# Input projections of a two-layer kernel in another order, and the gate's Silu in two halves

## The reference

```python
h = _rmsnorm(x, norm_w)
proj = jnp.einsum('bld,de->ble', h, w_in)
aq, ak, av, az, dq, dk, dv, dz, b_f, a_f, b_b, a_b = _split_proj(proj)
attn = _neighbourhood_attention(rms(aq), rms(ak), av, rpb) * jax.nn.silu(az)      # 8 heads of 64
qkv = jax.nn.silu(_centred_depthwise_conv(concat([dq, dk, dv]), conv_w))          # 4 heads of 128
o_f = _gated_delta_chunked(dq, dk, dv, g_f, beta_f)          # chunks, each with a triangular solve
o_b = flip(_gated_delta_chunked(flip(dq), flip(dk), flip(dv), flip(g_b), flip(beta_b)))
o = o_f + o_b
o = o * lax.rsqrt(jnp.mean(o * o, axis=-1, keepdims=True) + EPS) * dn_norm_w
delta = o * jax.nn.silu(dz)
x = x + jnp.einsum('ble,ed->bld', jnp.concatenate([attn, delta], axis=-1), w_out)
```

## Time and profile before

| what | us |
|---|---|
| median of 3 runs | 2304.66 (2299.58 to 2307.76) |
| span of the profiled execution | 2301.0 |
| from its start to the last input projection's end | 560.0 |
| from there to the first matmul of wo0, at 764.3 | 204.3 |
| from wo0's first matmul to the end | 1536.7 |

### The profile page before, as it was taken

How to read it: one execution, slowest core, us unless ns; L and a number is a source line. 1 busy time by engine, 2 the same in 40 slices (tenths; PEclk the granted TensorE clock), 3 DMA queues, 4 the chain that set the end, 5 groups by cost and what they waited for, 6 DMA issues and landing times.

```text
span 2301.0 us, 29061 instructions
## 1 busy us (share of the span) xinstructions
PE 2206.9 (96%) x11559; PEld 1800.5 (78%) x11559; DVE 1093.5 (48%) x2025; ACT 936.8 (41%) x1705; POOL 380.9 (17%) x596
## 2 busy tenths in 40 slices
PE   8999999898997899999999999999999999999998
PEld 6778777676796688788887788887888888888886
DVE  5454545443256343566555664655514243433441
ACT  4544544343364143456455554543313233232220
POOL 5200112644403110000000000003301111010111
PEclk9999999999598899999999999999999999999999
DMA  4621345353743231111110211112221111344232
GB/s 142 221 82 58 86 127 171 109 149 101 242 157 92 110 124 52 42 49 62 34 59 23 65 56 46 37 46 69 64 66 55 37 56 55 119 140 158 93 105 87
DMA packets 171384, 209.76 MB, mean 91 GB/s; under 512 B 36576, under 2 KB 124752, under 8 KB 169712
## 3 DMA queue, kind: packets, MB, share of 16 engines
q1 hardware_dynamic: 150752, 141.51, 19.6%
q0 software_dynamic: 20496, 66.39, 9.0%
HBM read 150.41 MB, written 53.77 MB: 89 GB/s over the span
## 4 chain that ended last, share of the span: by engine, by line
PE 86%; DVE 5%; ACT 4%; issue 1%; DMA 1%; POOL 1%; SPq 0%; DVEq 0%; POOLq 0%; ACTq 0%
PE PS L1730 12%; PE PS L1732 12%; PE PS L1731 12%; PE PS L1724 9%; PE PS L1726 9%; PE PS L1725 9%; PE PS L1690 5%; PE PS L2018 3%; PE PS L1997 3%; PE PS L1801 2%; PE PS L1827 2%; DVE WH L2439 2%; PE PS L2050 1%; PE PS L2063 1%; DMA RAW<-in_w_in 1%
## 5 line engine op out<-in xcount | busy, mean ns | idle before, releaser
L1730 PE MATMUL PS<-WH,HH 128*128 128x512 f32 x1344 | 546.8, 407 | 19.3 <-DVE WH L2439 10.7
L1732 PE MATMUL PS<-WH,HL 128*128 128x512 f32 x1344 | 528.1, 393 | 0.0
L1731 PE MATMUL PS<-WH,HH 128*128 128x512 f32 x1344 | 527.2, 392 | 0.0
L1724 PE MATMUL PS<-HH,WH 128*128 128x512 f32 (+1 forms) x976 | 399.5, 409 | 4.2 <-DVE WH L2439 4.2
L1726 PE MATMUL PS<-HH,WH 128*128 128x512 f32 (+1 forms) x976 | 382.9, 392 | 0.0
L1725 PE MATMUL PS<-HL,WH 128*128 128x512 f32 (+1 forms) x976 | 382.3, 392 | 0.0
L1730 PEld LDWEIGHTS PS<-WH,HH 128*128 128x128 f32 x1344 | 254.8, 190 | 78.8 <-DVE WH L2439 11.8
L1732 PEld LDWEIGHTS PS<-WH,HL 128*128 128x128 f32 x1344 | 254.0, 189 | 55.2
L2439 DVE SCALAR_TENSOR_TENSOR WH<-RAW,WK,WH 128x512 fp32r<-128x512 f32 (+2 forms) x248 | 188.0, 781 | 221.4 <-ACT WH L2072 220.8
L1731 PEld LDWEIGHTS PS<-WH,HH 128*128 128x128 f32 x1344 | 255.3, 190 | 46.2
L1724 PEld LDWEIGHTS PS<-HH,WH 128*128 128x128 f32 (+1 forms) x976 | 183.0, 187 | 43.7 <-DVE WH L2439 5.7
(11 more groups left out here) (313 smaller groups left out, 2923.2 us busy)
## 6 DMA issues: line engine op xcount, KB each, us to landing
RAW<-in_w_in SPq DMA_DIRECT2D x200, 256.0 KB, 2.9
RAW<-in_w_out SPq DMA_DIRECT2D x32, 256.0 KB, 3.5
sig_d<-WK POOLq DMA_DIRECT2D x32, 256.0 KB, 2.3
WK<-sig_d POOLq DMA_DIRECT2D x32, 256.0 KB, 3.2
WK<-in_rpb POOLq DMA_DIRECT2D x16, 480.0 KB, 5.6
RAW<-in_w_in SPq DMA_DIRECT2D x32, 192.0 KB, 2.6
dnc_d<-TM SPq DMA_DIRECT2D x12, 512.0 KB, 3.6
TM<-dnc_d SPq DMA_DIRECT2D x10, 512.0 KB, 4.6
```

The lines of the kernel that those rows point to most:

```text
L1724: e.matmul(ps, wh, hh, start=k == 0, stop=False)
L1730: e.matmul(ps, hh, wt[:, 0:width], start=k == 0, stop=False)
L1731: e.matmul(ps, hh, wt[:, 512:512 + width], start=False, stop=False)
L1732: mm = e.matmul(ps, hl, wt[:, 0:width], start=False, stop=k == 7)
```

## The change

The blocks come in the order dn0, dn1, dn2, dn3, na0, na1, na2, dz, na3. Delta head 0 is now the block whose six tiles run together. dz is evacuated by ACT with a plain scaled copy into TM[:, 2], the region where `solve` works, so it waits for the inverse's last stores; then Silu (ACT) and the norm weights (POOL) are applied in place to four tiles at a time, each half with one store. In the plan dz waits for ("da", 1). Pair 3's attention is set free only after na3, like the other pairs', and its V is gathered on POOL in one part.

```diff
-X = ["dz", "dn0", "dn1", "dn2", "na0", "dn3", "na1", "na2", "na3"]
+X = ["dn0", "dn1", "dn2", "dn3", "na0", "na1", "na2", "dz", "na3"]
+    def waiting(held):
+        return held and held[:2] == ("tile", 0) and ("g", *held[1:], 7) in plan.known and ("ev", *held[1:]) not in plan.known
-        if ring[state["n"] % len(ring)] == state["open"]:
+        while ring[state["n"] % len(ring)] == state["open"] or waiting(holder.get(ring[state["n"] % len(ring)])):
     def first_out(b):
-        for t in range(8):
-            yield has("xs")
-            yield has("g", b, t, 7)
-            slot(("ev", b, t), "stg", 3)
-            put("ev", b, t)
-            plan.now[0] += 1200.0
-            if t in (1, 3):
-                yield
-                put("xb", t // 2)
-            yield
-        put("dg")
+        yield has("xs")
+        for th in range(2):
+            put("xb", th)
+            yield
+        put("dg")
+        for c in range(3):
+            if c == 2:
+                yield has("co", 0, 0)
+            for th in range(2):
+                yield has("g", b, (c, th), 7)
+                put("ev", b, (c, th))
+                yield
+            plan.spawn(conv(0, c))
...
+                if b == 0:
+                    plan.drain(has("xb", 1))
+                put("ev", b, t)
...
-        if p == 3:
-            yield has("d9", 1, 14)
         if ("no", p, 1 - h, 7) in plan.known and ("nw", p) not in plan.known:
             put("nw", p)
...
+    def gate_side():
+        for half in range(2):
+            yield has("ev", BLOCK["dz"], 4 * half + 3)
+            put("zs", half)
+            yield
...
-        if name == "na3":
-            rows(3)
+        if name == "dz":
+            plan.drain(has("da", 1))
+            plan.spawn(gate_side())
         gemm(b)
...
-            if n < 3:
-                rows(n)
+            rows(n)
     def share():
         yield has("g", X_LAST, 7, 7)
-        yield has("nv", 3, 3, 1)
-        yield has("da", 0)
         plan.both(*((kind, h) for h in range(2) for kind in ("dl", "dv")), ("dt", 0), ("dt", 1))
-        yield has("nw", 2)
-        yield has("da", 1)
+        yield has("zs", 1)
         plan.both(("dl", 2), ("dv", 2), ("dt", 2))
...
                     if name == "dz":
-                        w.wait_ge(c_stg[i], 16 * n)
                         w.wait_ge(*at["xs", "r"])
-                        e.activation(stg[i], ps, ACT.Silu, scale=rs[:, 72 + t:73 + t]).then_inc(*w.sig(*item, "z"))
+                        w.wait_ge(c_im, 448)
+                        w.wait_ge(c_pa, 128)
+                        copy(gate_tile(t), ps, rs[:, 72 + t:73 + t]).then_inc(*w.sig(*item, "out"))
...
+                elif kind == "zs":
+                    half = a[0]
+                    z = gate_half(half)
+                    w.wait_ge(*at["ev", BLOCK["dz"], 4 * half + 3, "out"])
+                    e.activation(z, z, ACT.Silu).then_inc(*w.sig(*item, "z"))
+                    e.preload_act_table_set(LN_EXP)
```

More of the change, by code:

```diff
@@ L154, in slot_of @@
     return n % XSLOT if n < 8 * len(X) else n % NSLOT
-EV_READ = {"dz": "z", "na0": "ss", "na1": "ss", "na2": "ss", "na3": "ss"}
+EV_READ = {"na0": "ss", "na1": "ss", "na2": "ss", "na3": "ss"}
 COLS = ((0, 24, 0), (8, 32, 288), (24, 32, 288), (40, 24, 672))
@@ L316, in work @@
     if kind == "nv":
-        return [("pool", 2330)] if a[0] < 3 or a[2] and a[1] < 2 else [("dma", 3500)]
+        return [("pool", 2330)]
     if kind == "d9":
@@ L577, in na_gather @@
             yield has("ge")
[L578 to L581, removed]
-                yield
-        if p < 3:
-            put("nz", p)
+        yield has("ev", BLOCK[f"na{p}"], 7)
+        for g in range(4):
+            put("nv", p, g)
             yield
-            put("nx", p)
+        put("nz", p)
+        yield
+        put("nx", p)
     def table():
@@ L1177, in raw, with gate_tile, gate_half @@
             return TM[:, 2, n % 2 * 1024:(n % 2 + 1) * 1024]
+        def gate_tile(t):
+            return TM[:, 2, t * 512:(t + 1) * 512]
+        def gate_half(half):
+            return TM[:, 2, half * 2048:(half + 1) * 2048]
         def conv_out(n):
@@ L1414, in build @@
         c_tab = [semaphore(f"c_tab{i}") for i in range(NTAB)]
-        c_stg, c_oa = ([semaphore(f"{n}{i}") for i in range(3)] for n in ("c_stg", "c_oa"))
+        c_oa = [semaphore(f"c_oa{i}") for i in range(3)]
+        c_zst = semaphore("c_zst")
         c_ring, c_st, c_ot, c_dl, c_vx, c_at = (
@@ L1543, in _ @@
                         load(n)
[L1545 to L1551, removed]
                 elif kind == "nx":
@@ L2864, in _ @@
                     dma(tab[n % NTAB], rpb[n // 4 * 2 + n % 2, n // 2 % 2], c_tab[n % NTAB])
-                elif kind == "ev":
-                    b, t = a
-                    name = BLOCKS[b]
-                    if item in slots:
-                        i, n = slots[item]
-                        w.wait_ge(*at[(*item, "z")])
-                        w.wait_ge(c_dn, 80)
-                        z = stg[i].rearrange("p (h c) -> p h c", h=4)
-                        e.tensor_tensor(z, z, dnw.unsqueeze(1).to_broadcast([128, 4, 128]),
-                                        ALU.mult).then_inc(*w.sig(*item, "out"))
-                        w.wait_ge(*w.last)
-                        dma(dz_d[t * 128:(t + 1) * 128, :], stg[i], c_stg[i])
+                elif kind == "zs":
+                    half = a[0]
+                    z = gate_half(half).rearrange("p (h c) -> p h c", c=128)
+                    w.wait_ge(*at[(*item, "z")])
+                    w.wait_ge(c_dn, 80)
+                    e.tensor_tensor(z, z, dnw.unsqueeze(1).to_broadcast([128, 16, 128]),
+                                    ALU.mult).then_inc(*w.sig(*item, "m"))
+                    w.wait_ge(*w.last)
+                    dma(dz_d[half * 512:(half + 1) * 512, :].rearrange("(t p) c -> p t c", p=128),
+                        gate_half(half).rearrange("p (t c) -> p t c", t=4), c_zst)
                 elif kind == "ed":
@@ L2887, in _ @@
                         dma(out[t * 128:(t + 1) * 128, cb * 512:(cb + 1) * 512], ot[n_o % 4], c_ot[n_o % 4])
-                elif kind == "nv" and (a[0] < 3 or a[2] and a[1] < 2):
-                    p, g, part = a
+                elif kind == "nv":
+                    p, g = a
                     w.wait_ge(*at["ev", BLOCK[f"na{p}"], 7, "out"])
@@ L2897, in _ @@
                         w.wait_ge(*at["gt", 1, "t"])
-                        for cc, v in z_stores():
-                            w.wait_ge(cc, v)
-                    gather(dma, p, g, c_v3[1][g] if part else c_vg[g], slice(3, 4) if part else slice(0, 4))
+                    gather(dma, p, g, c_vg[g])
                 elif kind == "nw":
@@ L2953, in _ @@
                     h = a[0]
[L2954 to L2955 removed]
+                    w.wait_ge(c_zst, 32)
                     for done in na_read():
```

43 lines of the change are left out of this document (12 added, 31 removed).

## The result

| what | before | after |
|---|---|---|
| median, us | 2304.48 (2299.58 to 2307.76) | 2412.35 (2405.52 to 2416.06) |
| ratio to before | 1 | 1.048 [1.045, 1.051] |
| span of the profiled execution | 2301.0 | 2403.7 |
| first matmul of na0 | 186.8 | 225.5 |
| na2's end; gate's first, third tile | | 469.8; 530.2, 575.4 |

A forecast was written before the change was run, and what follows sets the result against it. The kernel was taken as bound by TensorE up to 560 us, with idle and half-rate time before 764.3. Projections ending at 574 plus 205 gave 779 to wo0, 15 later: 2319 us, range 2280 to 2342.

The forecast's parts named there:

- Amount of work: Whole kernel: every projection, attention item and recursion step stays, TensorE's work the same to within a microsecond.
- Start, 6 us within -1 to +12: First blocks: 6 us lost because few tiles lie before the norm sums; bounds -1 (narrower weights), +12 (nothing covers).
- dn3 ends where dn2 ended.: Delta blocks: equal tile counts assumed, so dn3 ends at 186.8 plus 6, 193 us.
- 5 of 16 outputs in na3: Within na3 before: 5 of 16 outputs of pair 3, with 8 of 16 scores, taken as 11 us.
- Pair 2 alone, 53 us: After na2: pair 2's attention runs without a projection beside it, at half rate, 53 us, to 483.
- Inverse's first load 25 us after dn3: After dn3: the triangular inverse's first load comes 25 us later (18 to 28), at 218.
- Inverse 272.7 plus 12, less 10 for a store no longer in its way: Inverse before dz: previous length plus 12, less about 10 for one attention store on POOL; ready at 493 (475 to 510).
- The two sides meet: Before dz's third tile: TensorE ready at 494, the inverse at 493, so the tile starts at about 494.
- After na3, 205 us: Projections' end to wo0: 88 us to the recursion's start, then 117; 205 against 204.3, bounds 165 and 219.
- C: Before dz: no wait, inverse ready by 470, pair 2's attention inside dz, projections end near 557; 2302 us, chance 0.14.
- D: Before dz: inverse takes longer, each microsecond above 494 costs TensorE one; at 519 it gives 2344 us; chance 0.13.
- B: After na3: granted clock stays at 1.00, recursion starts after 56 us instead of 88; 2282 us, chance 0.24.

The follow-up runs named there:

- e5: The changed kernel with POOL's zero fill made to wait for the norm sums of dn0's second convolution: 2402.04 us, ratio 1.042.
- e10: The changed kernel with pair 2's store put in the plan behind the second inverse's last POOL step: 2403.85 us, ratio 1.0423.
- e1: The kernel before with only dn3 moved ahead of na0, the gate still first: 2300.48 us, ratio 0.9997.
- e3: The changed kernel with only the zero fill moved in the plan behind dn1's first convolution: 2411.8 us, ratio 1.0486.
- e8: The changed kernel with the zero fill behind the first norm sums and 10 of 15 POOL steps of both inverses left out: 2383.0 us, ratio 1.0353.

## Why the prediction was wrong

- *Amount of work.* Right: wo0 to the end differs by 2.9 us, and na3 alone took 44.9 as forecast (43.7).
- *Start, 6 us within -1 to +12.* This step failed, and it is the largest error: 51.5 us for the same 26 tiles, 38.7 if read at na0. The forecast took both convolutions to start at about 55 and 13 us from first tap to norm sums; the first tap is at 75.6 and the sums at 97.5. The 13 us came from a stretch in which the gates' chain was not in the same queue of ACT. And the zero fill, which POOL had issued from 75.0 on and now issues from 53.5 on, just as dn1's weights load, was not costed at all (in e5 the first tap is at 57.7 and na0 13.7 earlier; 10 us in the time): the sum had followed compute items past their queues and left out a DMA. The bound of +12 took "nothing covers" to mean one chain's length.
- *"dn3 ends where dn2 ended."* A miscount: dz, dn0, dn1 and dn2 are 28 tiles' worth, dn0 to dn3 are 26. By the forecast's own terms dn3 would have ended near 180 (174.0 and 6), not 193, and the inverse would have been ready near 480, well before the 494 of TensorE. It ended at 225.6. (The 5 of 16 outputs in na3 are a slip too: the earlier trace rows has 52, so 4; it moves the sum by 1 us.)
- *Pair 2 alone, 53 us.* Right in mechanism, 60.4 in size, at a clock of 0.55 as in the earlier trace rows.
- *Inverse's first load 25 us after dn3.* Right: 26.7 (225.6 to 252.3).
- *Inverse 272.7 plus 12, less 10 for a store no longer in its way.* This step failed too. From first load to last step it took 311.4 us, 38.7 more than before and 48.7 more than the forecast had it. Pair 2's store did lie in its way, with two table loads: 21.0 us within the second inverse's steps. The item had been read as "one store fewer", without asking what stands on POOL between its steps in the new order; e10 prices the store at 12.9 us of wait. The greater part lies elsewhere, as the kernel before, e1 and after show in three stretches: from the first load until the first images have landed 185.6, 181.3 and 183.7 us; from there to the second inverse's first step on POOL 46.1, 66.7 and 72.0; from that to the first of its stores 41.0, 51.0 and 55.7. So most of the added length, 25.9 us, is in the loads and products ahead of POOL's steps, and 20.6 of it come with dn3's place alone (e1). What holds them up there was not taken apart.
- *"The two sides meet."* Wrong by the sum of these: third tile at 575.4 instead of 494. Only 32.2 us of the 81 are the wait for the inverse; TensorE's own side was 49 late. The forecast had taken two estimates of 494 and 493 with a spread of 20 and 35 and put the meeting at zero, where any error of either kind costs time.
- *After na3, 205 us.* Measured 209.4, but by luck: two terms missed in opposite directions. From the end of the projections to the recursion's first product, where the forecast had 88 us at half rate, the profiled execution took 76.7 at a mean clock of 0.84; from there to wo0 132.8 instead of 117. In e3, e5 and e10, whose projections end in the same order, the first stretch took 98.3, 91.2 and 90.4 us at 0.55 to 0.64, so the half rate of the forecast is there in three of four profiles and not in this one.
- *Rivals.* C fell. D named the true direction. With its images at 573, 79 late, its rule of a microsecond of TensorE for each of the inverse gives 2398, but it comes near the time by luck: of those 79 only 32 were TensorE waiting for the inverse. It was carried to 519 only and had 0.13. B's condition was met in the profiled execution, where the clock was full for over half of the stretch after na3 (0.84 in the mean), and not in e3, e5 and e10; its price fell: the recursion began after 76.7 us, not 56.

As a sum of profiles: 15 was forecast to wo0 and 99.8 came. Of the difference, 85, the start makes 45.5 (51.5 less 6), the wait 32.2, pair 2 alone 7.4, what follows na3 4.4 and the gate's first two tiles, at half rate, 2.0. The stretch from the 27th tile to na2's end took 5.7 less than forecast (244.3 against 250), and the tiles behind the wait 0.7 less.

## What to carry over

Where a new order makes one tile wait for another engine's chain, write down everything that this engine's queue holds between the chain's steps in the new order, transfers included: a store that waits for the very work that TensorE does ahead of the tile ties the two ends together, and no shortening of the chain undoes it. Before two orders are compared at the start of a block, count the work that stands ahead of it in each: at na0 they seemed 38.7 us apart, for equal work it was 51.5. Moving an item later in a list moves nothing in time if its engine has nothing to wait for (e3), and a block moved to the front brings its side items with it: here the norm sums, the gates' chain and the fill came together in dn1. A forecast that rests on two chains meeting should be priced at the later of two uncertain ends, not at the gap between their means.

## What the hardware showed unexpectedly

**A busy TensorE at half rate.** Busy time of e8 within pair 2's attention alone:

```profile
500.00:520.00 20.00, 20.00 (x74) 16.00 (x74) 3.71 (x20) 4.90 (x12) 4.37 (x11) 0.50 0.19 56
```

TensorE is busy for 20.00 of 20 us and the granted clock is 0.50, 1.2 GHz. The Trainium skill, "TensorE: Matmul & The Clock Gate", Part 1 (the HAM clock gate), has a busy array run at full rate; this row disagrees, as the earlier trace rows did, if "busy" is what the profile counts, which includes the modelled ends of matmuls. On the gate's third tile in after the rule holds: its matmuls of 512 columns start 0.43 us apart up to 578.1 and 0.23 us apart from 578.5 on, 1.2 and then 2.4 GHz.

**The same work, at two clocks.** From the end of the projections to wo0, in after and then in e3, which on the chip ran the same order:

```profile
654.70:864.10 209.40, 162.51 (x1797) 142.80 (x1797) 106.49 (x285) 100.88 (x277) 43.99 (x63) 0.84 0.45 151
```

```profile
654.50:886.20 231.70, 191.18 (x1797) 166.93 (x1797) 106.66 (x285) 101.80 (x277) 44.15 (x63) 0.70 0.41 136
```

1797 matmuls in both, the same start, idle 46.9 and 40.5 us, but a mean clock of 0.84 and 0.70, and 22.3 us between them, 21.6 of which lie before the recursion's first product (76.7 against 98.3). The profiled execution of after was the fastest of its four. e5 and e10 read 0.73 in profile (225.9 and 225.0 us), and this took back their 16 us of earlier projections there; their medians, which hold several executions, keep 10 and 8.5. So wo0's time in one profile of this family is uncertain by some 20 us, and what an edit moves is better read at the projections' end and in the medians. What decides the clock in that stretch from one execution to the next is open.

**A fill that starves small loads.** Six DMAs of zeros held the 16 DMA engines at a share of 1.02 (393 GB/s), and a wait of 11.4 us for weights on another queue was the result; with the fill later (e5) the share was 0.48 and that wait was gone. In the kernel before, the same fill at a share of 0.93 cost TensorE nothing, so what it costs depends on what loads beside it.
